# Scan output map 512 columns wide, its last pieces block by block, router on the transposed residual, expert rows gathered from the residual

## The reference, cut to what matters

```python
gy = _rms_norm(gy, norm_w.reshape(N_GROUPS, D_INNER // N_GROUPS)).reshape(b, l, D_INNER)
yx = gy @ w_out
x = x + mx[2] * _rms_norm(yx, norm_w[i, 1])
hx = _modulate(_rms_norm(x, norm_w[i, 2]), mx[3], mx[4])
...
logits = (t @ router_w).astype(jnp.float32)          # t = hx
top_v, top_i = lax.top_k(logits, TOP_K)
gates = jax.nn.softmax(top_v, axis=-1)
...
for e in range(N_EXPERTS):
    out = out + combine[:, e:e + 1] * _swiglu(t, w_gu[e], w_down[e])
```

## Time and profile before

| what | us |
|---|---|
| median of 3 runs (2137.31 to 2140.82) | 2137.99 |
| the profiled execution, whole time | 2139.38 |
| its span | 2137.6 |
| PE busy in the span | 1952.6 (91%) |
| DVE busy | 1474.9 (69%) |
| ACT busy | 1278.8 (60%) |

### The profile page before, as it was taken

How to read it: one execution, slowest core, us unless ns; L and a number is a source line. 1 busy time by engine, 2 the same in 40 slices (tenths; PEclk the granted TensorE clock), 3 DMA queues, 4 the chain that set the end, 5 groups by cost and what they waited for, 6 DMA issues and landing times. The chain is left out here.

```text
span 2137.6 us, 30845 instructions
## 1 busy us (share of the span) xinstructions
PE 1952.6 (91%) x11333; PEld 1628.3 (76%) x11334; DVE 1474.9 (69%) x1683; ACT 1278.8 (60%) x1790; POOL 150.9 (7%) x124
## 2 busy tenths in 40 slices
PE   3989889999997888787668999999999999999996
PEld 3967778888876767666666788888888888888885
DVE  2155463223466857667556989898989989898987
ACT  4235473222455345545456778787878888888875
POOL 0000000000000245444100000000000000000100
PEclk7999999999999899899788999999999999999998
DMA  9349723322444312211165999999999999999994
GB/s 321 119 171 383 275 79 99 99 99 99 158 169 132 100 40 80 60 59 60 44 202 200 339 345 388 344 390 348 378 373 354 387 338 392 344 384 351 375 394 157
DMA packets 251299, 503.89 MB, mean 236 GB/s; under 512 B 10347, under 2 KB 71099, under 8 KB 251195
## 3 DMA queue, kind: packets, MB, share of 16 engines
q1 hardware_dynamic: 250619, 500.36, 65.0%
q0 software_dynamic: 576, 2.10, 0.3%
HBM read 497.71 MB, written 4.72 MB: 235 GB/s over the span
## 5 line engine op out<-in xcount | busy, mean ns | idle before, releaser
L1888 DVE TENSOR_TENSOR lo<-raw,hi 128x1024 fp32r<-128x1024 f32 x844 | 1020.6, 1232 | 356.6 <-ACT hi L1384 254.4
L1402 ACT ACTIVATE hi<-raw 128x1024 fp32r<-128x1024 f32 x672 | 709.5, 1063 | 180.6 <-PE bank L768 173.9
L766 PE MATMUL bank<-hi,xh_t 128*128 128x512 f32 (+1 forms) x1248 | 463.0, 371 | 23.5 <-DVE lo L1888 14.6
L767 PE MATMUL bank<-lo,xh_t 128*128 128x512 f32 (+1 forms) x1248 | 459.9, 368 | 0.0
L768 PE MATMUL bank<-hi,xl_t 128*128 128x512 f32 (+1 forms) x1248 | 459.5, 368 | 0.0
L1384 ACT ACTIVATE hi<-raw 128x1024 fp32r<-128x1024 f32 x132 | 139.4, 1066 | 292.3 <-PE bank L986 172.6
L766 PEld LDWEIGHTS bank<-hi,xh_t 128*128 128x128 f32 x1248 | 239.2, 192 | 65.6 <-issue 21.5
L768 PEld LDWEIGHTS bank<-hi,xl_t 128*128 128x128 f32 x1248 | 239.3, 192 | 38.4
L767 PEld LDWEIGHTS bank<-lo,xh_t 128*128 128x128 f32 x1248 | 239.4, 192 | 37.4
L766 PE MATMUL bank<-hi,hth 128*128 128x512 f32 x624 | 249.1, 399 | 1.4 <-DVE lo L1888 0.7
L768 PE MATMUL bank<-hi,htl 128*128 128x512 f32 x624 | 244.0, 391 | 0.0
(11 more groups left out here) (304 smaller groups left out, 2153.3 us busy)
## 6 DMA issues: line engine op xcount, KB each, us to landing
raw<-in_moe_gu_w_dram SPq DMA_DIRECT2D x224, 1024.0 KB, 7.7
raw<-in_moe_down_w_dram SPq DMA_DIRECT2D x112, 1024.0 KB, 7.3
raw<-in_ada_w_dram SPq DMA_DIRECT2D x24, 2048.0 KB, 9.4
raw<-in_ffn_gu_w_dram SPq DMA_DIRECT2D x22, 1024.0 KB, 5.0
raw<-in_ffn_down_w_dram SPq DMA_DIRECT2D x22, 1024.0 KB, 4.9
raw<-in_ssm_in_w_dram SPq DMA_DIRECT2D x16, 1024.0 KB, 5.3
raw<-in_mix_out_w_dram SPq DMA_DIRECT2D x8, 1024.0 KB, 11.4
raw<-in_ssm_out_w_dram SPq DMA_DIRECT2D x8, 1024.0 KB, 5.5
```

The source lines that it names most:

```text
L766: mm(o, a_hi, w_hi, start=first, stop=False, **kw)
L767: mm(o, a_hi, w_lo, start=False, stop=False, **kw)
L1402: A_(hi[:, p % SPL, :], raw[:, u, (p % 2) * PIECE:(p % 2 + 1) * PIECE], ACT.Copy).then_inc(m_hi, 1)
L1888: TT(lo[:, p % SPL, :], raw[:, u, h * PIECE:(h + 1) * PIECE], hi[:, p % SPL, :].bitcast(F32), ALU.subtract).then_inc(done, 1)
```

## The change

1. The output map's units become 512 output columns by 512 rows of `w_out`, in the order `SSM_OUT` of pairs (group of rows, half of columns): (0,0), (1,0), (0,1), (1,1), (2,0), (2,1), (3,0), (3,1). A piece then is 2 row tiles by 512 columns: 6 matmuls of 512 columns for each block instead of 12 of 256. Group 3 is first needed at unit 6 instead of in the second half of unit 4. `late` for group 3 moves from before unit 3 to before unit 4. The last four pieces (units 6, 7) are run for block 0 first and then for block 1. Each block and half has its own bank.
2. `post_out(b)` replaces copy, post-norm and residual add, in halves of 512 columns: ACT squares straight from the bank, DVE copies the bank, scales and adds.
3. The router no longer uses the normed, modulated rows. The residual itself is transposed (`rows_t`), and multiplied in plain fp32 by router weights that are scaled by the modulation's columns (`rwa`); the row's 1/rms is applied to the eight logits, and the shift's part of them (`lgc`) comes from eight matmuls over a broadcast column of `ada`.
4. The gather takes rows of `xres`; the selection matrix holds 1/rms in place of 1. Gather, modulation and split go in two halves, and PE may start an expert's first unit on the first half.
5. On DVE the work that the gather doesn't need (gates, counts, second-round places, the splits of pieces 1 to 3 of expert 0) stands behind `slots`. ACT's `grow_out` waits for `gf_done` 4, and its `hi_to` bounds are one to three pieces further.

```diff
@@ -610,12 +617,14 @@
                                      (drow, A["ssm_d"][0])):
                         sp.dma_start(dst, src.partition_broadcast(P)).then_inc(ld_ssm, 16)
             for i in range(2 * U_MIXOUT):
-                kh, q = divmod(i, U_MIXOUT)
+                kq, half = SSM_OUT[i]
                 if i == RAW // 2:
                     sp.wait_ge(yy_t, N_GROUPS * NQ)
                 if i == RAW // 2 + 1:
                     sp.wait_ge(gn_t, N_GROUPS)
-                load_cols(S_SSMOUT + i, A["ssm_out_w"][0][kh * D_MODEL:(kh + 1) * D_MODEL, :], q * UCOL)
+                u = unit_of_split(S_SSMOUT + i)
+                load(u, "split", S_SSMOUT + i, rawv(u, 4),
+                     wcols(A["ssm_out_w"][0][kq * 4 * P:(kq + 1) * 4 * P, :], half * 512, 512))
             sp.wait_ge(gf_done, 4)
             sp.dma_start(rw, A["router_w"][0].rearrange("(t p) n -> p t n", p=P)).then_inc(ld_rw, 16)
 
...
@@ -1156,20 +1165,22 @@
                                    stop=(d == 1 and hp % 2 == 1 and b == 1 and last), skip_group_check=True)
                 m.then_inc(yy_t, 1)
 
-            def ssm_out(i, h):
-
-                kh, q = divmod(i, U_MIXOUT)
+            def ssm_out(i, h, blocks=LAT):
+
+                kq, half = SSM_OUT[i]
                 p = 2 * (S_SSMOUT + i) + h
-                pe.wait_ge(gf_done, 2 * kh + h + 1)
+                pe.wait_ge(gf_done, kq + 1)
                 pe.wait_ge(lo_ready, p + 1)
-                for b in LAT:
-                    for t in range(4):
-                        k = 8 * kh + 4 * h + t
-
-                        m = tok3(bank[q][:, b * UCOL:(b + 1) * UCOL], xh16[:, k, b * P:(b + 1) * P],
-                                 xl16[:, k, b * P:(b + 1) * P], *wpart(p, t, UCOL),
-                                 first=(k == 0 and b == 0), last=(k == 15 and b == 1), group=False)
-                m.then_inc(piece_used, 1)
+                for b in blocks:
+                    for t in range(2):
+                        k = 4 * kq + 2 * h + t
+                        m = tok3(out_bank(b, half)[:, :], xh16[:, k, b * P:(b + 1) * P],
+                                 xl16[:, k, b * P:(b + 1) * P], *wpart(p, t, 512),
+                                 first=(k == 0), last=(k == 15))
+                if blocks[-1] == LAT[-1]:
+                    m.then_inc(piece_used, 1)
+                elif h == 1:
+                    m.then_inc(so_half, 1)
 
             def project(g, k):
                 if g == N_GROUPS:
...
@@ -1227,36 +1238,58 @@
                     scan(g, k)
 
             pe.wait_ge(sg_ready, N_GROUPS * NQ)
-            for i in range(2, 2 * U_MIXOUT):
-                if i == 3:
+            for i in range(2, 6):
+                if i == 4:
                     late(N_GROUPS - 1, 2)
                 for h in range(2):
                     ssm_out(i, h)
-                if i == U_MIXOUT:
...
+            for b in LAT:
+                for i in (6, 7):
+                    for h in range(2):
+                        ssm_out(i, h, (b,))
+
+            def rows_t(b, half):
+
+                pe.wait_ge(*((po_done, 9 + b) if half else (x_half, b + 1)))
+                pe.wait_ge(grow_ready, 5 + b)
+                for k in range(4 * half, 4 * half + 4):
+                    m = pe.transpose(bank[4 + 2 * b + half][:, (k % 4) * P:(k % 4 + 1) * P],
+                                     xres[:, b, k * P:(k + 1) * P], ident)
+                m.then_inc(rx_t, 1)
+
+            def logits(b):
+
+                for k in range(KC):
+                    if k % 4 == 0:
+                        pe.wait_ge(*((rx_dve, 1) if b == 1 and k == 4 else (rx_act, 2 * b + k // 4 + 1)))
+                    m = mm((bank[0], bank[4])[b][:, 0:8], xT[b][:, k, :], rwa[:, k, :], start=(k == 0), stop=(k == KC - 1))
+                m.then_inc(lg_t, 1)
+
+            rows_t(0, 0)
+            rows_t(0, 1)
+            pe.wait_ge(ld_rw, 16)
+            pe.wait_ge(o_sq, 3)
+            pe.wait_ge(o_ev, 3)
             for k in range(KC):
...
+                m = mm(bank[1][:, 0:8], ada[:, 1, 24 + k, 0:1].to_broadcast((P, P)), rw[:, k, :],
+                       start=(k == 0), stop=(k == KC - 1))
+            m.then_inc(lg_const, 1)
+            rows_t(1, 0)
+            pe.wait_ge(rw_scaled, 1)
+            logits(0)
+            rows_t(1, 1)
+            logits(1)
             pe.wait_ge(rt_v, 1)
...
+            mm(bank[1][:, 0:8], strict, mask[:, 0, :], start=True, stop=True)
+            mm(bank[1][:, 8:16], strict, mask[:, 1, :], start=True, stop=False)
+            mm(bank[1][:, 8:16], ones, mask[:, 0, :], start=False, stop=True).then_inc(rt_t, 1)
+            mm(bank[5][:, 0:8], ones, mask[:, 0, :], start=True, stop=False)
+            mm(bank[5][:, 0:8], ones, mask[:, 1, :], start=False, stop=True).then_inc(rt_cnt, 1)
 
 
             def mpiece(p, a):
...
@@ -1310,9 +1345,10 @@
                 pe.wait_ge(slot_ready, it + 1)
                 for k in range(KC):
                     for b in range(2):
-                        m = mm(bank[2 + k // 4][:, (k % 4) * P:(k % 4 + 1) * P], mxn[b][:, k * P:(k + 1) * P],
+                        m = mm(bank[2 + k // 4][:, (k % 4) * P:(k % 4 + 1) * P], xres[:, b, k * P:(k + 1) * P],
                                slot1[:, b, :], start=(b == 0), stop=(b == 1))
-                m.then_inc(gat_t, 1)
+                    if k % 4 == 3:
+                        m.then_inc(gat_t, 1)
 
             def combine(it, c, b):
...
@@ -1775,45 +1811,74 @@
                         late(g - 1, k)
                     scan(g, k)
             late(N_GROUPS - 1, 1)
-            hi_to(2 * S_SSMOUT + 4 + SPL)
+            hi_to(2 * S_SSMOUT + 7 + SPL)
             late(N_GROUPS - 1, 3)
             norm_rms(3, 4)
-            hi_to(2 * S_SSMOUT + 6 + SPL)
+            hi_to(2 * S_SSMOUT + 9 + SPL)
             norm_hi(3)
-            hi_to(2 * S_SSMOUT + 8 + SPL)
-            for q in range(U_MIXOUT):
-                p = 2 * (S_SSMOUT + U_MIXOUT + q)
...
+            hi_to(2 * S_SSMOUT + 10 + SPL)
+            act.wait_ge(gf_done, 4)
+            for r in (4, 5):
+                grow_out(r)
+            hi_to(P_MOE)
+
+            def out_square(b, half):
+
+                if b == 0:
+                    act.wait_ge(so_half, half + 1)
+                else:
+                    act.wait_ge(piece_used, P_MOE - 2 * (1 - half))
+                c = 26 + 2 * b + half
+                A_((mpjunk, yexp)[b][:, half * 512:(half + 1) * 512], out_bank(b, half)[:, :], ACT.Square,
+                   accum_out=ss[:, c:c + 1]).then_inc(o_sq, 1)
+
...
+            out_square(0, 0)
+            out_square(0, 1)
+            out_rms(8)
             hi_moe(0, 0, True)
+            out_square(1, 0)
+            out_square(1, 1)
+            out_rms(9)
+            row_rms(0)
+            rows_copy(0, 0)
+            rows_copy(0, 1)
             hi_moe(1, 0, True)
-            norm_b(12)
-            norm_b(13)
+            rows_copy(1, 0)
+            row_rms(1)
...
             def gather_mod(it):
 
-                act.wait_ge(gat_t, it + 1)
                 a_, b_ = mod_cols(3, 0)
                 for k in range(KC):
+                    if k % 4 == 0:
+                        act.wait_ge(gat_t, 2 * it + k // 4 + 1)
                     i = A_(mt32[:, k * P:(k + 1) * P], bank[2 + k // 4][:, (k % 4) * P:(k % 4 + 1) * P],
...
+            def post_out(b):
+
+                n = 8 + b
+                for half in range(2):
+                    dve.wait_ge(o_sq, 2 * b + half + 1)
+                    dve.tensor_copy(yout[:, b, half * 512:(half + 1) * 512], out_bank(b, half)[:, :]).then_inc(o_ev, 1)
+                c = 26 + 2 * b
+                TT(ss[:, 14 + n:15 + n], ss[:, c:c + 1], ss[:, c + 1:c + 2], ALU.add).then_inc(po_ss, 1)
+                dve.wait_ge(po_rms, n + 1)
+                dve.reciprocal(rstd[:, 14 + n:15 + n], rms[:, 14 + n:15 + n]).then_inc(po_rstd, 1)
+                dve.wait_ge(po_rstd, n + 1)
+                dve.wait_ge(o_ev, 2 * b + 2)
+                dve.wait_ge(grow_ready, 5)
+                for half in range(2):
+                    o = slice(half * 512, (half + 1) * 512)
+                    STT(mptmp[:, o], yout[:, b, o], rstd[:, 14 + n:15 + n], mgrow[0][:, o], ALU.mult, ALU.mult).then_inc(ph_t, 1)
+                    dve.wait_ge(ph_t, 2 * b + half + 1)
+                    TT(xres[:, b, o], xres[:, b, o], mptmp[:, o], ALU.add).then_inc(po_done if half else x_half, 1)
...
@@ -2298,66 +2381,54 @@
                 for k in range(SLOTS):
                     scan(g, k)
             gated(N_GROUPS - 1)
-            lo_to(2 * S_SSMOUT + 4 + SPL)
+            lo_to(2 * S_SSMOUT + 7 + SPL)
             norm_ab(3)
-            lo_to(2 * S_SSMOUT + 6 + SPL)
+            lo_to(2 * S_SSMOUT + 9 + SPL)
             norm_lo(3)
-            for i in range(6, 16):
-                lo_to(2 * S_SSMOUT + i + 1 + SPL)
+            lo_to(P_MOE)
```

(47 more changed lines are left out.)

122 lines of the change are left out of this document (49 added, 73 removed).

## The result

| kernel | median of the runs, us | lowest to highest | profiled execution: time, span |
|---|---|---|---|
| before | 2138.74 | 2137.31 to 2140.82 (4) | 2139.38, 2137.6 |
| changed | 2125.72 | 2124.21 to 2127.24 (4) | 2125.23, 2123.4 |

Changed to before: 0.9939 with an interval of 0.9924 to 0.9955. The change made the kernel 13.0 us faster; I had forecast 19.0, and 2125.72 lies just outside the range that ended at 2125.5.

What follows compares the result with a forecast made beforehand. PE bounds the experts, so the first expert product's start counts: output map +4.3, hand-over -23.6, feed +0.3, together -19.0 us from 2137.99 to 2119.0; range 2112.5 to 2125.5.

Steps and rivals of the forecast that it cites:

- Part 1: Output map: matmuls of 512 columns instead of 256 give 2.3 us less work over 16 pieces.
- Part 2: Output map: the new order loses time; last output product at 1102.7 instead of 1098.4, 4.3 us later.
- A: Output map: from a scan product ahead of its last pieces to the start of its last product; forecast 67.9 us.
- Part 3: Hand-over from output map to first expert product: 41.4 us to 17.75, -23.6; plain fp32 products at 0.15 each.
- T0: End of the output map for block 0, from which the hand-over is counted; forecast at 1097.3 us.
- (b): Output map and hand-over: clock lost more often, output piece p7 +2.7, `late` +0.5; another half-clock stretch +5, 2124; 12%.
- Part 4: Experts: two added DVE operations per expert, about 0.2 us, fit in 8.8 us of idle DVE and cost nothing.
- the feed: First expert: PE waits a little for the split of piece 4; 0.3 us lost.
- C: Experts and after: from the first expert product to the kernel's end; forecast 998.1 us.
- (a): Output map: small slip, the clock stays up over waits, `late` and p8 at full speed; 2115.3, at best 2112.5; 15%.
- (c): Start of the experts: transfers become the bound, two units of 2.75 us lost; 2124.5; 8%.
- (d): Experts: halves put DVE behind at the gather's split, 3.5 us stall at each of seven boundaries; 2143.5; 4%.

## Why the prediction was wrong

**Part 1, the wide map: right.** 2.55 us measured alone, 2.05 without the shorter wait, against 2.3. The row's spacings decided rightly. The Trainium skill (TensorE: Matmul & The Clock Gate, "Wait — 56ns, not 53.3ns?") gave 0.5 us by its fixed cost of about 2.5 ns; the measurement differs and decides.

**Part 2, the output map: right, in time and in cause.** A was 67.58 for 67.9; p8 began within 0.1 us of the forecast, at the lower clock, held by unit 4's transfer, and moving `late` gave it back. Some luck is in the 0.1 us: p7 had the half clock in place of `late` (1.89 us, full clock), so `late` ended 0.7 us later than forecast, and unit 4 was there 0.6 us sooner behind it (7.5 us for 8.1).

**Part 3, the hand-over: this is the step that failed, in the term "Plain fp32 products of 8 columns aren't in the trace as such ... I take 0.15".** The 12 products on the path were to cost 0.15 us each, at most 0.18. They cost 0.43 at the level of 1.2 GHz, and not 12 but all 16 stood on the path, as leaving half of them out showed. I read the gather's row as 32 products in 5.80 us; they are 16 products of two instructions, so 0.36 each, as the loop (eight chunks, two blocks) says. The number of columns does not help: at full clock instructions start 0.112 us apart with 8 columns as with 128, so a product takes 0.22. Corrected for the count alone, the sum would be 12 x 0.07 = 0.8 us longer.

The trace gives the place of each part. From block 1's residual to its last logits the forecast had 3.4 us, and the trace has 7.2: PE ends block 0's products 2.9 us behind the residual, transposes for 0.9 and needs 3.4 for block 1's. That is 3.8 us more. To the selection matrix it was 0.8 more, with the rank sums at the lower level, and from there to the first expert product 1.0 more, with the gather's first half at the lower level. The residual itself came 0.2 sooner: +5.4 from T0 on, which is 5.2 from the last output product on.

The rest beside the count is the clock. I had given its loss a chance of 12% in rival (b), with p7 and `late` as its places. The transposes' price of 0.23 us was read from a row at the lower level, and the gather's row lay in a stretch at 0.74, but the narrow products I priced as if the level did not enter. With the gaps filled, at full clock, the hand-over took 17.28 us: the selection matrix was ready at T0 + 17.6 (forecast 17.5), and the gather's first half came sooner than forecast. So without the lower level the forecast would have held within 0.9 us; the level is worth the 6.1 us from 17.28 to 23.38. The block-by-block order (4.85 us) and the halves of the gather (1.99 us) paid as worked out.

**Part 4 and the feed: near in the sum, and part of it wrong.** From first to last expert product it was 976.6 us for the 978 forecast (977.9 before), and C is 1.3 us shorter than before, not 0.3 longer. The two profiles compare well, since both lost the level at the wait in expert 0. Before, the first eight expert products ran at the lower level; now they run at full clock, which gives 1.6 us. Against that, the two DVE operations more per expert were not "nothing": PE waits 0.36 to 0.46 us for a split at each of seven boundaries, and the distance from one expert's gather to the next is 121.76 us for some 121.55, 1.2 us in all. The trace shows the place: near the second boundary DVE's four half operations take 2.13 us (1365.88 to 1368.01) where two whole ones took 1.86 before (1380.05 to 1381.91), and right behind them stands the split for which PE waits. The mean idle time of DVE, from which I took the term, doesn't tell when DVE is idle. Behind the last gather the experts are 1.2 us shorter than before, and no run tests why. PE's longest wait for a split was 1.9 us, as before.

**The rivals.** (a) did not come, the clock was lost. (b) is what happened in kind, 2124 against 2125.7; it had p7 right, but the larger loss came at another place. (c) is out, since C did not grow. (d)'s mechanism is there, at 0.2 us a boundary instead of 3.5. The range missed by 0.2 us: it allowed for one more half-clock stretch of 5 us, where the earlier trace rows already had such a stretch in the hand-over before.

The loss behind waits is what the Trainium skill describes (TensorE: Matmul & The Clock Gate, "HAM oscillation — how this bites in real kernels"). The traces agree for p7 (behind 3.12 us), for p8 (behind 7.51 us) and for `late` (behind 5.72 us in one run). They also show a loss in the hand-over with gaps of 0.5 to 0.7 us ahead of it and one with no gap, and behind one wait of 1.9 us in the experts both outcomes.

## What to carry to other kernels

Where a chain of small steps hands over between engines, price every product on it at both clock levels; the low one is the likelier (every profile here whose gaps were left open had it over most of the hand-over). Count instructions, not products: plain fp32 takes two for each, with 8 columns as with 128. And where PE waits for a known time on such a chain, products that nobody reads can pay (11 of them took 8.0 us off the median here, 6.1 in the hand-over and 1.7 in the experts, where the level held at the wait of 1.9 us, which may be chance), but measure it again, in several runs, after every change ahead of them. And don't take room for an added operation from an engine's mean idle time: look at the place where its result is waited for.

## What the runs showed of the hardware

- A plain fp32 product with 128 rows and columns of weights is two matmul instructions. From start to start one takes 0.112 us at full clock and 0.213 at half, with 8 moving columns as with 128. So the columns do not set it. The load of the weights, 128 columns in all of them, is what is left; no run varies it. The Trainium skill (TensorE: Matmul & The Clock Gate, "LDWEIGHTS (loading the stationary operand)") has 128/1.2 = 107 ns for a load of 128 columns; the trace is 5% above that at full clock, and at half clock it took twice that.
- The granted clock fell to 0.50 within 5 us behind over 20 us of dense work, with gaps of 0.51 and 0.69 us between small products, and with no gap at all between them in another order. Filling the gaps kept 1.00 in three profiles of three at one place, and did not in two of two some 8 us earlier, behind the same sequence.
- Behind the same wait of 1.86 to 1.89 us in the first expert, with the same work for tens of us ahead of it, eight profiles of 17 lost the level for some 3.4 us and nine kept it. That is the larger part of the 2 us by which C differs: 994.7 to 995.1 us in the nine, 996.4 to 997.8 in the eight.
